# A decoder step on one core: the prompt's rows are loaded ahead of W_in's first quarter, and each query moves inside a z tile

## What is computed

```
z  = x @ w_in                       # 1024 -> q | k | v | B | C | h, 512 columns each
att  = moba_attend(q, k, v)         # 8 heads x 64; samples: the 3 best of 8 past blocks of 256 keys, by page table
conv = B * dwconv3_causal(C * h)
x1 = LayerNorm(alpha * x + concat(att, conv) @ w_out)
u  = dwconv3_causal(x1 @ w_ffn_up);  a, g = split(u)
y  = LayerNorm(alpha * x1 + (silu(a) * g) @ w_ffn_down)
```

## Time and profile before

| | us |
|---|---|
| median of 3 runs | 440.23 (439.62 to 440.43) |
| the profiled execution | 439.81 |
| its span | 438.0 |
| TensorE busy | 412.9 (94%) |
| VectorE busy | 295.2 (67%) |
| ScalarE busy | 181.2 (41%) |
| GpSimd busy | 106.5 (24%) |

### The profile page before, as it was taken

How to read it: one execution, slowest core, us unless ns; L and a number is a source line. 1 busy time by engine, 2 the same in 40 slices (tenths; PEclk the granted TensorE clock), 3 DMA queues, 4 the chain that set the end, 5 groups by cost and what they waited for, 6 DMA issues and landing times.

```text
span 438.0 us, 8235 instructions
## 1 busy us (share of the span) xinstructions
PE 412.9 (94%) x2903; PEld 339.1 (77%) x2903; DVE 295.2 (67%) x382; ACT 181.2 (41%) x694; POOL 106.5 (24%) x133
## 2 busy tenths in 40 slices
PE   5999999999999998999999989999999999999990
PEld 5588887876866774765554479999999999999990
DVE  0498999999799976954441274667766776534437
ACT  1587469644378233112110234544455555233201
POOL 1004134995255221100000707122211221000002
PEclk9999999999999999999999999999999999999996
DMA  8999999899999999999999933655566665667002
GB/s 316 393 362 407 405 407 378 323 393 408 410 353 364 354 400 405 405 405 404 404 402 402 353 113 97 193 172 160 162 179 194 196 194 179 190 202 215 2 1 99
DMA packets 109515, 124.86 MB, mean 285 GB/s; under 512 B 5775, under 2 KB 66920, under 8 KB 109466
## 3 DMA queue, kind: packets, MB, share of 16 engines
q1 hardware_dynamic: 101138, 107.56, 69.9%
q10 hardware_dynamic: 8336, 16.78, 10.2%
HBM read 121.90 MB, written 2.61 MB: 284 GB/s over the span
## 4 chain that ended last, share of the span: by engine, by line
PE 57%; DVE 18%; SPq 9%; issue 6%; DMA 5%; POOL 2%; ACT 1%; DVEq 0%; POOLq 0%; ACTq 0%
PE ps L1807 11%; PE ps L1808 11%; PE ps L1809 11%; SPq L352 7%; DVE qk L929 6%; DVE T L939 5%; PE ps L1700 4%; PE ps L1424 4%; PE ps L1619 4%; PE ps L1595 3%; PE ps L1621 3%; PE ps L1371 3%; DMA wring<-in_cache_v 2%; DMA KV<-in_cache_k 2%; POOL x1l L603 1%
## 5 line engine op out<-in xcount | busy, mean ns | idle before, releaser
L1176 DVE TENSOR_TENSOR wlo<-KV,whi 128x2048 fp32r<-128x2048 f32 (+1 forms) x24 | 61.8, 2575 | 57.1 <-ACT whi L829 29.1
L1424 PE MATMUL ps<-xT,wring 128*128 128x264 f32 x384 | 89.6, 388 | 0.1
L1424 PEld LDWEIGHTS ps<-xT,wring 128*128 128x128 f32 x384 | 71.6, 190 | 13.5 <-issue 1.7
L1807 PE MATMUL ps<-x1h,whi 128*128 128x264 f32 x256 | 73.7, 288 | 0.2
L1808 PE MATMUL ps<-x1l,whi 128*128 128x264 f32 x256 | 72.6, 284 | 0.0
L1809 PE MATMUL ps<-x1h,wlo 128*128 128x264 f32 x256 | 72.5, 283 | 0.0
L929 DVE TENSOR_TENSOR qk<-KV,qk 128x1536 f32<-128x1536 f32 (+1 forms) x32 | 67.5, 2111 | 5.7 <-DMA KV<-in_cache_k 2.2
L660 ACT ACTIVATE qk<-qk 128x64 f32<-128x64 f32 x216 | 51.8, 245 | 29.7 <-POOL qk L551 21.6
L939 DVE TENSOR_REDUCE T<-qk 128x24 f32<-128x1536 f32 (+1 forms) x32 | 58.4, 1827 | 0.0
L1807 PE MATMUL ps<-fh,whi 128*128 128x264 f32 x176 | 50.3, 286 | 0.1
L1808 PE MATMUL ps<-fl,whi 128*128 128x264 f32 x176 | 49.9, 284 | 0.0
(11 more groups left out here) (213 smaller groups left out, 572.4 us busy)
## 6 DMA issues: line engine op xcount, KB each, us to landing
KV<-in_cache_k SPq DMA_DIRECT2D x128, 256.0 KB, 6.5
KV<-in_w_ffn_up SPq DMA_DIRECT2D x32, 512.0 KB, 4.7
KV<-in_cache_v SPq DMA_DIRECT2D x60, 256.0 KB, 7.9
wring<-in_cache_v SPq DMA_DIRECT2D x56, 256.0 KB, 6.9
KV<-in_w_ffn_down SPq DMA_DIRECT2D x8, 1408.0 KB, 6.4
wring<-in_w_in ACTq DMA_DIRECT2D x5, 2048.0 KB, 14.1
zbuf<-in_cache_v SPq DMA_DIRECT2D x12, 256.0 KB, 5.2
zbuf<-in_w_ffn_up SPq DMA_DIRECT2D x3, 1024.0 KB, 10.3
```

The source lines that it names most:

```text
L1176: nc.vector.tensor_tensor(wlo[s][:, 0:n], w2[s][:, 0:n], whi[s][:, 0:n], ALU.subtract).then_inc(s_lo, 1)
L1424: ins = nc.tensor.matmul(ps[:, z_bank(n), 0:R], tile[k], xT[:, k, :], start=k == 0, stop=k == KT - 1)
L1807: nc.tensor.matmul(out, wh[k], xh[k], start=k == 0, stop=False)
```

## The change

It has four parts, all in the first 50 us.

- The prompt's rows are issued first on ScalarE's queue, and W_in's first quarter in their place on SyncE's, behind four small loads.
- TensorE warms with 5 matmuls, turns all eight groups of the prompt's rows, warms with 5 more, and only then takes the query product.
- Each query is spread by a matmul in the middle of a z tile (after four of its eight matmuls): query n inside tile n. The state's transposes stand behind tile 5 instead of tile 3.
- ScalarE issues W_in's second quarter as soon as the query product is done, ahead of the queries' copies. Its order is query, z tile, sums, for each j; the state's copies stand behind the sums of group 5.

```
-WARM = 14
+WARM = 5
...
-            sp.dma_start(rows, x_prompt[0].rearrange("(r p) d -> p r d", p=P)).then_inc(s_x, 16)
+            sp.dma_start(wring[:, 0, :].rearrange("p (k n) -> p k n", k=KT),
+                         win[:, :, Z_ORDER[0] * DA:(Z_ORDER[0] + 1) * DA]).then_inc(s_win[0], 16)
...
-            load_win(0)
+            act.dma_start(rows, x_prompt[0].rearrange("(r p) d -> p r d", p=P)).then_inc(s_x, 16)
...
-            for k in range(6):
+            for k in range(KT):
                 x_copy(k)
-            query(0)
-            x_copy(6)
-            x_copy(7)
+            act.wait_ge(s_qsps, 1)
             load_win(1)
-            query(1)
-            sum_products(0)
-            for j in range(1, 4):
-                z_tile(j - 1)
-                query(2 * j)
-                query(2 * j + 1)
+            for j in range(3):
+                query(j)
+                z_tile(j)
                 sum_products(j)
+            query(3)
             z_tile(3)
             load_win(2)
+            sum_products(3)
+            for j in range(4, 6):
+                query(j)
+                z_tile(j)
+                sum_products(j)
...
-            for j in range(4, 8):
-                sum_products(j)
-                z_tile(j)
+            query(6)
+            z_tile(6)
+            sum_products(6)
+            query(7)
+            z_tile(7)
             load_win(3)
+            sum_products(7)
...
-            for i in range(WARM):
-                nc.tensor.matmul(ps[:, 5, 0:P], ident, ident, start=True, stop=True)
+            def warm():
+                for i in range(WARM):
+                    nc.tensor.matmul(ps[:, 5, 0:P], ident, ident, start=True, stop=True)
+
+            warm()
...
             pe.wait_ge(s_x, 16)
-            for k in range(4):
+            for k in range(KT):
                 x_transposes(k)
+            warm()
             pe.wait_ge(s_xsP, 1)
             pe.wait_ge(s_win[0], 16)
...
-            for k in range(4, 6):
-                x_transposes(k)
-            pe.wait_ge(s_qs, 3)
 
             def query(b):
-                if b >= 2:
+                if b == 0:
+                    pe.wait_ge(s_qs, 3)
+                elif b >= 2:
                     pe.wait_ge(s_qb, b - 1)
...
-            query(0)
-            x_transposes(6)
-            x_transposes(7)
-            query(1)
-            for n in range(3):
-                z_tile(n)
-                query(2 * n + 2)
-                query(2 * n + 3)
-            z_tile(3)
+            for n in range(6):
+                z_tile(n, lambda: query(n))
...
-            z_tile(4)
-            z_tile(5)
-            z_tile(6)
-            z_tile(7)
+            z_tile(6, lambda: query(6))
+            z_tile(7, lambda: query(7))
```

## The result

| | before | changed |
|---|---|---|
| median | 440.23 us (5 runs, 439.62 to 441.15) | 443.95 us (5 runs, 442.93 to 444.31) |
| ratio | | 1.0076, 95% interval 1.0059 to 1.0093 |
| the profiled execution / its span | 439.81 / 438.0 | 444.31 / 442.5 |

The change makes the kernel slower by 3.7 us. The forecast, 441.4 (439.2 to 443.4), was too low. That it would be slower was its likeliest sign, but that this came true is luck: the mechanism for which it said so didn't take place. The trace is read in the same order as before.

A forecast was written before the change was run, and what follows sets the result against it. VectorE's key-page scan, then TensorE's penalty matmul and the value transfers, were taken to bound the kernel. Only the third-quarter key squeeze cost anything: span 438.0 + 1.2 = 439.2, median 440.23 + 1.2 = 441.4, range 439.2 to 443.4.

The forecast's parts named there:

- the costing of TensorE's start: TensorE up to the first query: z tiles start at 16.4, first multiply at 19.3, 1.2 us later, at no cost.
- rival 3: TensorE's array stays at half speed through the prompt's transposes: scan starts at 23.3, +3.2 us, 443.4; chance 0.06.
- The forecast's own sign of being wrong: VectorE's scan: the forecast is wrong if group 6 starts at 43.4 without a wait, or group 4 well before 34.
- The free 1.99 us: VectorE waited 1.99 us for group 4's keys, so up to that much later start of the scan costs nothing.
- From there the scan has no slack to recover in: VectorE's scan after group 7: the lateness of group 6 stays to the end, +1.2 us.
- The squeeze by W_in's third quarter: Quarter issued at 31.2, not 34.77, stretches the keys' time by 2.1; group 6 lands 1.2 us late: +1.2, chance 0.48.
- group 4's keys stay at 34.5: Both kernels have moved the same bytes through full engines by 34.5 us, so group 4's keys land no later.
- What TensorE's lead is worth: TensorE's lead of 2.5 to 3.5 us at z tile 7 ends waiting for the row copy at 67.57: 0.
- rival 4: Rows or W_in's quarter land after TensorE asks; each microsecond past 14.5 delays the query, 0.8 free; chance 0.04.
- The second quarter's wait: ScalarE issues W_in's second quarter after the query product, at 16.4; the first query's copy, due at 18.1, loses nothing.
- The state's copies and taps: State's copy ends near 47 instead of 37.5, GpSimd's taps 9.5 us later, just covered by 9.54 us idle: 0.
- Rival 1: Group 4's keys land by 33.2 and full speed comes early; the scan gains up to 1.35 us: 438.9, chance 0.15.

The follow-up runs named there:

- after_w14_5: The changed kernel with 14 warming matmuls instead of 5 ahead of the prompt's transposes, and 5 behind them as it has: 442.36 us, ratio 1.0039.
- before_w5: The kernel before with 5 warming matmuls instead of 14 and nothing else changed: 441.81 us, ratio 1.0030.
- after_w14_0: The changed kernel with 14 warming matmuls ahead of the prompt's transposes and none behind them: 443.87 us, ratio 1.0078.
- before_loads: The kernel before with only the loads exchanged: prompt's rows first on ScalarE's queue, W_in's first quarter in their place on SyncE's: 440.50 us, ratio 1.0006.
- after_keep: The changed kernel with 12 identity matmuls, result unread, in TensorE's idle time ahead of row block 2's transposes: 443.49 us, ratio 1.0061.
- before_keys4: The kernel before with group 4's keys issued ahead of the state's loads and group 5's ahead of the constants: 441.02 us, ratio 1.0023.

## Why the prediction was right or wrong

**The step that failed** is the costing of TensorE's start: "Two groups of transposes at half speed (1.0 each) go to 10.3, six at 0.51 to 13.4, ten warming passes at 0.11". All eight groups and all ten passes were at the lower level. It is rival 3, which had 6 in 100. The argument against it was that transposes without idle time keep the array as busy as warming matmuls do. For raising the clock it is wrong: 6.5 us of them didn't (9.10 to 15.60), while with nine more matmuls ahead, in after_w14_5, the clock was up when they began. In before_w5 the five matmuls and the wait behind them didn't raise it either. What was true, and was read from the earlier trace rows, is only that transposes didn't lower a clock that had already risen. Rival 3's own numbers came close: scan at 23.3 (measured 23.64), +3.2 at group 4 (+3.77), 443.4 (443.95). A group at half speed was put at 1.0 and took 0.82, and the rise came late in the product instead of ahead of it.

The first multiply was forecast at 19.3 and came at 23.64. Of these 4.3 us the transposes are 1.4 (6.50 instead of 5.1), the second warming 1.3 (2.43 instead of 1.1), and the product 0.8 (2.67 instead of 1.9): 3.5 for the clock. The first warming took 0.2 more than reckoned (2.30 instead of 2.1), and 0.6 is x_sample's rows, which land later with the exchanged loads (5.88 instead of 5.28); the forecast began its sum at 6.20 as before and left that out.

The forecast's own sign of being wrong, group 6 without a wait for keys, came true (46.63, 0.20). One slip in rival 3 changes little: 8.3 + 8 x 1.0 is 16.3, not 16.5.

**The free 1.99 us** at group 4 held: 5.55 us of later start became 3.77 there (5.55 - 1.99 = 3.56, and 0.20 for the engine's usual pause, which stood inside the 1.99).

**"From there the scan has no slack to recover in"** held roughly up to group 14: +3.77 at group 4, +3.26 at group 6, +3.7 at group 14. Then VectorE's wait for TensorE, which no term had, made it 5.7.

**The squeeze by W_in's third quarter**, the forecast's one paid term (+1.2), did not take place, since z tile 3 ended late and the quarter left at 36.16, not at 31.2. Where it left at 33.0 (after_w14_0), group 6's keys came at 44.7. By the forecast's working with group 4's keys at 34.5 (33.0 + 4.1 + 2.6 x 2.1) they were due at 42.6. But group 4's keys came 1.24 later there (35.79), and with that the working gives 37.1 + 3.84 x 2.1 = 45.2, close to what was measured. So its factor fits; what failed there is "group 4's keys stay at 34.5". In before_loads the exchange alone moves them by 0.5.

**What TensorE's lead is worth** was put at 0, since it would be spent in the wait for the row copy at row block 2, grown "from 1.01 to some 3 us". The wait grew to 2.60, and to 3.39 in after_w14_0. But 0 was wrong: behind this idle time the clock could fall, which the text priced at nothing and no rival named. Filling it took 2.4 us off the median of after_w14_0; in the changed kernel's profile it stands ahead of VectorE's new wait of 1.73.

**The loads** landed as predicted (6.2; 11.5, and 11 to 12.5 was said) and hid behind the transposes; rival 4 did not happen. **The second quarter's wait** cost nothing, but its purpose was missed, since it left at 20.85 instead of 18.36. **The state's copies and taps** cost nothing: page group 9's product on GpSimd at 55.95 waited for ScalarE's sum alone.

**Rival 1, the keys sooner,** did not happen in this change. Its idea was sound with another edit: moving the constants behind the keys gave -0.9 us.

How the 3.7 us are made up, as far as runs show it: 1.6 is the missing warming ahead of the transposes (443.95 to 442.36, one edit). The other 1.9, which after_w14_5 still has without slow transposes and without a fall in its profile, is not split by any time. At group 4 that kernel is 2.3 late. Without the second warming 1.1 of it goes (0.4 of this because the clock rose sooner in that profile), the old order takes 0.6, and of the 0.7 that is left the exchanged loads are 0.5 by before_loads. But these are starts in single profiles and no shares of the time: without the second warming the time got worse, and the exchanged loads alone cost nothing. What the fall at 70 us adds stays open (443.95 against 443.49 in after_keep, within the noise).

## What to carry to other kernels

Here transposes without idle time didn't raise TensorE's clock, though they ran on at the higher level once it was up. So work that raises the clock has to be told apart from work that merely keeps it: before cutting a warm-up, look for the place where the passes change their distance, and what ran just before. A lead given to an engine that will wait for something anyway isn't free if its idle time changes the clock behind it; put the saved time elsewhere, or fill the gap. And where a scan waits for transfers at full rate, what helped was to order the bytes by when they are needed (0.9 us), not to ask for the first result sooner (nothing).

## What the runs showed of the hardware that was not expected

- 6.5 us of float32 transposes without idle time (9.10 to 15.60) left TensorE at its lower level; the same kernel with nine more warming matmuls ahead did them at the higher one.
- A stall of 2.60 or 3.39 us had a granted clock of 0.57 behind it, and stalls of 2.76 us (after_w14_5) and 2.51 us (before_keys4) had 1.00. So its length alone doesn't decide, and what does stays open. In the changed kernel the clock was down before the stall ended (0.50 from 71 us, the stall ended at 71.47); in after_w14_0 the stall ended at 69.56, and the clock still read 1.00 from 70 to 71 us and 0.50 from 72 on, in the middle of busy work.
- The clock rises at another moment in each execution: 28 warming passes took 4.56 us in one profile and 6.00 in another.
- At a kernel's start the granted clock reads 1.00 while the passes are at half speed; only their distance shows it (0.21 against 0.11 us). The window of the changed kernel's transposes:

```profile
9.10:15.60 6.50, 6.50 (x25) 3.66 (x24) 0.00 (x0) 2.73 (x7) 0.00 (x0) 1.00 1.05 406
```

- With prompt's rows first on ScalarE's queue instead of W_in, x_sample's 8 rows on the other queue landed some 0.5 us later, although the load in front had half the bytes: TensorE, which waits for them, starts at 5.88 to 6.08 in the seven profiles with the exchanged loads and at 5.28 to 5.73 in the six without. Why isn't shown.
